# Two transformer blocks on one core: the wide projections turned from stationary to streaming weights

## What is computed

```python
h = rmsnorm(x, norm_g)                              # block 1
# attentions A (6 heads), C (4 heads), B (12 heads) give oa, oc, ob
g_a, g_b, g_c = split(sigmoid(h @ w_in[mix] + gate_bias), 3)
merged = g_a*(oa @ w_up_a) + g_b*(ob @ w_up_b) + g_c*(oc @ w_up_c)
x = x + merged @ w_o
h = concat([meta, x])                               # block 2, 16 + 256 tokens
u = rms_norm(h, g_pre_mix)
z_pool, v_conv, g_conv, gate_a, gate_b = split(u @ w_in_2)
y_a = pool(z_pool) @ w_pool_out                     # windows, a map per group
y_b = silu(layer_norm(conv31(v_conv * sigmoid(g_conv)))) @ w_conv_out
m = sigmoid(gate_a) * y_a + sigmoid(gate_b) * y_b
h = h + rms_norm(m @ w_o_2, g_post_mix)
u = rms_norm(h, g_pre_mlp)
h = h + rms_norm(square(relu(u @ w_up)) @ w_down, g_post_mlp)
```

## Time and profile before

| | us |
|---|---|
| median of 3 runs | 2298.14 (2297.1 to 2298.61) |
| profiled execution | 2297.23 |
| its span, first to last instruction | 2295.3 |
| PE busy | 2132.9 (93%) |
| PE weight loads | 1824.2 (79%) |
| DVE busy | 1590.3 (69%) |
| ACT busy | 966.8 (42%) |
| POOL busy | 418.4 (18%) |
| DMA | 384.46 MB, 167 GB/s |

### The profile page before, as it was taken

One profiled execution on the slowest core, in us unless ns is written; L12 is line 12 of the kernel. 1 busy time (PEld: TensorE's weight loads), 2 busy tenths in 40 slices (PEclk: granted clock), 3 DMA queues, 4 the chain that ended last, 5 costly groups with the idle time before them and its releaser, 6 DMA issues.

```text
span 2295.3 us, 33520 instructions
## 1 busy us (share of the span) xinstructions
PE 2132.9 (93%) x11733; PEld 1824.2 (79%) x11733; DVE 1590.3 (69%) x1828; ACT 966.8 (42%) x1197; POOL 418.4 (18%) x332
## 2 busy tenths in 40 slices
PE   6899999899998999799896999997999999999997
PEld 5767788788776888699775888776888888888886
DVE  6796876867876665646999867758645655655654
ACT  5443344566553444333232354445333333333343
POOL 3010010100213111102799402214000000000001
PEclk8899999999999999899998999998999999999999
DMA  7744555455446565355444545553556566556552
GB/s 233 223 124 139 149 165 160 133 155 166 138 138 188 169 202 186 122 181 157 139 148 133 175 137 183 183 183 128 183 192 189 186 192 193 183 193 192 185 185 89
DMA packets 345188, 384.46 MB, mean 167 GB/s; under 512 B 12359, under 2 KB 308213, under 8 KB 344679
## 3 DMA queue, kind: packets, MB, share of 16 engines
q1 hardware_dynamic: 341756, 370.95, 52.4%
q0 software_dynamic: 1120, 7.86, 1.0%
q10 hardware_dynamic: 2203, 4.23, 0.5%
HBM read 378.64 MB, written 4.23 MB: 167 GB/s over the span
## 4 chain that ended last, share of the span: by engine, by line
PE 67%; DVE 15%; POOL 8%; issue 5%; ACT 3%; DMA 1%; SPq 0%; DVEq 0%; POOLq 0%; ACTq 0%
PE acc L482 27%; PE acc L481 14%; PE acc L462 5%; PE acc L464 5%; PE acc L463 5%; DVE w_low L414 4%; POOL product L703 4%; PE acc L478 2%; POOL conv L705 2%; ACT w_high L406 2%; PE acc L472 2%; PE acc L474 2%; PE acc L473 2%; DVE tmp L499 2%; DVE conv L1735 1%
## 5 line engine op out<-in xcount | busy, mean ns | idle before, releaser
L414 DVE TENSOR_TENSOR w_low<-stage,w_high 128x1024 fp32r<-128x1024 f32 (+2 forms) x598 | 734.9, 1241 | 437.9 <-ACT w_high L406 423.8
L406 ACT ACTIVATE w_high<-stage 128x1024 fp32r<-128x1024 f32 (+2 forms) x598 | 606.0, 1023 | 749.9 <-PE acc L482 641.0
L482 PE MATMUL acc<-hT,w_high 128*128 128x512 f32 x1395 | 501.1, 398 | 0.0
L481 PE MATMUL acc<-hT,w_low 128*128 128x256 f32 x1395 | 406.3, 291 | 3.3 <-DVE w_low L414 3.3
L482 PE MATMUL acc<-u,w_high 128*128 128x512 f32 x960 | 344.9, 401 | 0.0
L482 PEld LDWEIGHTS acc<-hT,w_high 128*128 128x128 f32 x1395 | 264.8, 190 | 59.0 <-issue 3.4
L481 PEld LDWEIGHTS acc<-hT,w_low 128*128 128x128 f32 x1395 | 266.4, 191 | 18.0 <-issue 11.5
L481 PE MATMUL acc<-u,w_low 128*128 128x256 f32 x960 | 271.5, 283 | 1.8 <-DVE u L1374 1.8
L414 DVE TENSOR_TENSOR low_rows<-stage_rows,high_rows 128x1024 fp32r<-128x1024 f32 x128 | 158.6, 1242 | 156.8 <-ACT high_rows L406 156.4
L406 ACT ACTIVATE high_rows<-stage_rows 128x1024 fp32r<-128x1024 f32 x128 | 135.7, 1060 | 205.5 <-PE acc L464 177.3
L482 PEld LDWEIGHTS acc<-u,w_high 128*128 128x128 f32 x960 | 181.9, 189 | 42.3
(11 more groups left out here) (350 smaller groups left out, 3640.0 us busy)
## 6 DMA issues: line engine op xcount, KB each, us to landing
stage<-in_w_in SPq DMA_DIRECT2D x296, 512.0 KB, 3.7
stage<-in_w_up SPq DMA_DIRECT2D x128, 512.0 KB, 3.7
stage_rows<-in_w_down SPq DMA_DIRECT2D x128, 512.0 KB, 4.4
stage<-in_w_o SPq DMA_DIRECT2D x64, 512.0 KB, 4.5
stage<-in_w_mem_kv SPq DMA_DIRECT2D x16, 512.0 KB, 7.5
stage<-in_w_pool_out SPq DMA_DIRECT2D x16, 512.0 KB, 3.5
stage<-in_w_conv_out SPq DMA_DIRECT2D x16, 512.0 KB, 4.2
stage<-in_w_up_a SPq DMA_DIRECT2D x16, 384.0 KB, 3.3
```

Source lines behind the costliest of these rows:

```text
L406: act.activation(high[:, pr, 0:kt, 0:p.cols], src[:, slot, 0:kt, 0:p.cols], ACT.Copy).then_inc(high_done, 1)
L414: dve.tensor_tensor(low[:, pr, 0:kt, 0:p.cols], src[:, slot, 0:kt, 0:p.cols], high[:, pr, 0:kt, 0:p.cols].bitcast(F32), ALU.subtract).then ...
L481: pe.matmul(bk[:, 0:T], low, a, start=False, stop=False, skip_group_check=True)
L482: mm = pe.matmul(bk, high, both, start=False, stop=final, skip_group_check=True)
```

## The change

All gates, up-projections, w_o, w_pool_out, w_conv_out and w_o_2 take the form by rows, 512 columns a part (`by_rows`). Their products now lie with tokens on partitions:

- The bias of the mix gates varies along the row. POOL fetches it broadcast to 128 partitions, 512 columns at a time into a ring of two (`load_bias`); DVE adds it, ACT takes the sigmoid, DVE multiplies by the up-projection and adds. POOL has no merge left. Block 2's gates go from PSUM through ACT's sigmoid, scaled per token.
- merged, h1, m and h2 are needed by channels for the next matmul. PE transposes them, 8 pieces per row block (`turn_rows`, tables `MERGED_AT`, `RESIDUAL_AT`, `MIXED_AT`), and ACT and DVE split them out of PSUM (`high_turned` and `low_turned`; with the gain, `high_scaled` and `low_scaled`).
- A norm is one scalar per token on its partition: ACT squares a row block and accumulates. Block 2's first norm is applied after the products: values, gates and pools are multiplied by `rstd_bc`, which PE spreads from two diagonal matrices.
- x is read again from its input (no `spill_x`), g_post_mix and g_post_mlp are read as rows, two parameter loads at the start go, and the residual stays in rows to the end.
- Heads in w_up_a come every 4 slabs instead of 5, as the job has 44 slabs, not 48.

The diff, cut to its core:

```diff
-ROWS0 = [("gate_bias", 48), ("norm_g", 16), ("mem_norm_g", 16), ("g_pre_mix_2", 16), ("g_post_mix_2", 16), ("g_pre_mlp_2", 16)]
-ROWS1 = [("g_post_mlp_2", 16), ("pool_scale_2", 8), ("b_dw_2", 8), ("conv_ln_g_2", 8), ("conv_ln_b_2", 8), ("kv_norm_g", 2),
+ROWS0 = [("norm_g", 16), ("mem_norm_g", 16), ("g_pre_mix_2", 16), ("g_pre_mlp_2", 16)]
...
-                   "w_up_a": {5 + 5 * h: 6 + h for h in range(8)},
+                   "w_up_a": {4 + 4 * h: 6 + h for h in range(8)},
                    "w_up_c": {3 + 4 * h: 14 + h for h in range(8)}}
-        META_AT = 8
+        META_AT = 4
+        UP_B, HEADS_END = 11, 44
+        MERGED_AT = {"w_up_b": {UP_B * r + 12: r for r in range(3)}, "w_o": {1: 3}}
+        RESIDUAL_AT = {"w_o": {8 * r + 9: r for r in range(3)}, "values": {0: 3}}
+        SQUARES_AT = {"w_o": {8 * r + 8: r for r in range(3)}, "values": {0: 3}}
+        MIXED_AT = {"conv_out": {4 * r + 5: r for r in range(3)}, "w_o_2": {1: 3}}
...
+        def by_rows(w, col0, slabs, lhs, ready=None):
+            return Part(w, col0, slabs, None, ready, cols=ROW, stride=ROW, rows=lhs)
...
-        for w, b, slabs, before in (("w_up_a", 0, [3, 3], 0), ("w_up_c", 2, [2, 2], 3), ("w_up_b", 1, [3, 3], 5)):
-            order.append((w, Job(8, [Part(A["w_in"], MIX + b * D, full, rhs_of(hT)),
-                                     Part(A[w], 0, slabs, rhs_of(o_pair), ("o_split", before))], 4)))
-        order += [
-            ("w_o", Job(8, [Part(A["w_o"], 0, full, rhs_of(merged_pair), ("merged_ready", 0))], 2)),
-        ]
+        for w, b, slabs, before in (("w_up_a", 0, 3, 0), ("w_up_c", 2, 2, 3), ("w_up_b", 1, 3, 5)):
+            order.append((w, Job(4, [by_rows(A["w_in"], MIX + b * D, [2] * 8, hT),
+                                     by_rows(A[w], 0, [2] * slabs, o_pair, ("o_split", before))], 4)))
+        order.append(("w_o", Job(4, [by_rows(A["w_o"], 0, [2] * 8, merged_pair, ("merged_ready", 0))], 2)))
...
-            ("conv_gates", Job(8, [Part(A["w_in_2"], POOL_W + 2 * CONV_W + D, full, u_tokens)], 2)),
+            ("conv_gates", Job(4, [by_rows(A["w_in_2"], POOL_W + 2 * CONV_W + D, [2] * 8, u_rows)], 2)),
             ("pool_grp", Job(4, [Part(A["w_pool_grp_2"], 0, [2], rhs_of(d_pair), ("d_ready", 0), stride=0)], 8)),
-            ("pool_out", Job(8, [Part(A["w_in_2"], POOL_W + 2 * CONV_W, full, u_tokens),
-                                 Part(A["w_pool_out_2"], 0, [4, 4], rhs_of(y_pair), ("y_pair_ready", 0))], 4)),
-            ("conv_out", Job(8, [Part(A["w_conv_out_2"], 0, [4, 4], rhs_of(conv_pair), ("conv_ready", 0))], 4)),
-            ("w_o_2", Job(8, [Part(A["w_o_2"], 0, full, rhs_of(m_pair), ("m_ready", 0))], 2)),
+            ("pool_out", Job(4, [by_rows(A["w_in_2"], POOL_W + 2 * CONV_W, [2] * 8, u_rows),
+                                 by_rows(A["w_pool_out_2"], 0, [2] * 4, y_pair, ("y_pair_ready", 0))], 4)),
+            ("conv_out", Job(4, [by_rows(A["w_conv_out_2"], 0, [2] * 4, conv_pair, ("conv_ready", 0))], 4)),
+            ("w_o_2", Job(4, [by_rows(A["w_o_2"], 0, [2] * 8, m_pair, ("m_ready", 0))], 2)),
...
-            pool.dma_start(spill_x, turned[:]).then_inc(s("x_out"), 16)
...
+            def load_bias(n):
+                branch, r = (0, 2, 1)[n // 4], n % 4
+                if n < 2:
+                    pool.wait_ge(s("head_stats"), NORMS_ALL)
                 else:
-                    repeat(pool, job.steps, 1, body, link, 1 if add else 0)
+                    pool.wait_ge(s("gate_in"), 2 * (n - 1))
+                cols = slice(branch * D + r * ROW, branch * D + (r + 1) * ROW)
+                pool.dma_start(bias_ring[:, n % 2, :], A["gate_bias"][cols].partition_broadcast(P)).then_inc(s(f"bias_in{n % 2}"), 16)
...
+            def high_scaled(pair, q, bank, first_col, gain, turned_sem, done):
+                act.wait_ge(s(turned_sem), q + 1)
+                for a in range(2):
+                    k = 2 * q + a
+                    act.activation(pair[:, k, 0, first_col:first_col + T], aux[:, bank, a * T:(a + 1) * T], ACT.Copy,
+                                   scale=column(gain, k)).then_inc(s(done), 1)
...
+            def residual_squares(name, n):
+                r = SQUARES_AT[name].get(n)
+                if r is None:
+                    return
+                for t in range(2):
+                    e = 2 * r + t
+                    act.wait_ge(s("h1_rows"), e + 1)
+                    if e >= 2:
+                        act.wait_ge(s("h1_squared"), e - 1)
+                    act.activation(square[:, t, 0:ROW], h_rows[:, t, r * ROW:(r + 1) * ROW], ACT.Square,
+                                   accum_out=sums_1[:, t, r:r + 1]).then_inc(s("h1_squared"), 1)
...
+            def turn_rows(rows, q, bank, done):
+                for a in range(2):
+                    k = 2 * q + a
+                    for t in range(2):
+                        mm = pe.transpose(aux[:, bank, (2 * a + t) * P:(2 * a + t + 1) * P], rows[:, t, k * P:(k + 1) * P], ident[:])
+                mm.then_inc(s(done), 1)
...
+                if n == 2:
+                    pe.wait_ge(s("diag"), 3)
+                    pe.matmul(aux[:, 1, 0:META], ones[0:META, :], meta_diag[:], start=True, stop=True)
+                    for t in range(2):
+                        mm = pe.matmul(aux[:, 1, META + t * P:META + (t + 1) * P], ones[:], diag[:, t, :], start=True, stop=True)
+                    mm.then_inc(s("rstd_spread"), 1)
...
+            def turn_h2(r):
+                pe.wait_ge(s("h2_rows"), 2 * r + 2)
+                for q in (2 * r, 2 * r + 1):
+                    if q >= 4:
+                        pe.wait_ge(s("pair_ready"), 24 + q - 3)
+                    turn_rows(h_rows, q, q % 4, "h2_turned")
...
+            def low_scaled(pair, q, bank, first_col, gain, high_sem, first):
+                dve.wait_ge(s(high_sem), 2 * q + 2)
+                for a in range(2):
+                    k = 2 * q + a
+                    ins = dve.scalar_tensor_tensor(out=pair[:, k, 1, first_col:first_col + T], in0=aux[:, bank, a * T:(a + 1) * T], scalar=column(gain, k),
+                                                   in1=pair[:, k, 0, first_col:first_col + T].bitcast(F32), op0=ALU.mult, op1=ALU.subtract)
+                    link.put(ins)
+                dve.wait_ge(dve_link, link.n)
+                dve.sem_inc(s("pair_ready"), 1)
...
+                    if part == 0:
+                        dve.wait_ge(s(f"bias_in{n % 2}"), 16 * (n // 2 + 1))
+                        if n:
+                            dve.wait_ge(s("sig_ready"), 2 * n)
+                        for t in range(2):
+                            dve.tensor_tensor(tmp[:, t, 0:ROW], banks[:, t, :], bias_ring[:, n % 2, :], ALU.add).then_inc(s("gate_in"), 1)
+                        dve.wait_ge(s("gate_in"), 2 * n + 2)
+                        dve.sem_inc(acc_free, 1)
+                        return
+                    dve.wait_ge(s("sig_ready"), 2 * n + 2)
+                    for t in range(2):
+                        if n0 == 0:
+                            dve.tensor_tensor(merged[:, t, cols], banks[:, t, :], gate[:, t, 0:ROW], ALU.mult).then_inc(s("gate_used"), 1)
+                        else:
+                            link.put(dve.tensor_tensor(gate[:, t, 0:ROW], banks[:, t, :], gate[:, t, 0:ROW], ALU.mult))
...
+                    for t in range(2):
+                        dve.tensor_tensor(merged[:, t, cols], merged[:, t, cols], gate[:, t, 0:ROW], ALU.add).then_inc(s("gate_used"), 1)
...
-                dve.wait_ge(s("residual"), g + 1)
-                fold(dve, tmp[:, u, 0:2 * T].rearrange("p (a t) -> p a t", a=2), banks).then_inc(s("folded"), 1)
-                dve.wait_ge(s("folded"), g + 1)
+                r = 2 * i + u
+                cols = slice(r * ROW, (r + 1) * ROW)
+                if r == 0:
+                    dve.wait_ge(s("x_back"), 16)
+                for t in range(2):
+                    dve.tensor_tensor(h_rows[:, t, cols], banks[:, t, :], x_rows[:, t, cols], ALU.add).then_inc(s("h1_rows"), 1)
...
-            dve.wait_ge(s("residual"), 2 + 8)
-            inverse_std(TM, 1.0 / D, EPS)
-            normalize(lambda k: h1[:, k, :], uT, TM, "g_pre_mix_2", 16, rstd[:, 0:TM])
...
+                if n == 0:
+                    dve.wait_ge(s("h1_squared"), 8)
+                    link(dve.tensor_reduce(rs_1, sums_1, AX, ALU.add))
+                    dve.tensor_scalar(rs_1, rs_1, 1.0 / D, EPS, ALU.mult, ALU.add).then_inc(s("var_1"), 1)
+                if n == 1:
+                    dve.wait_ge(s("root_1"), 1)
+                    dve.reciprocal(rs_1, rs_1).then_inc(s("rs_1"), 1)
+                    dve.wait_ge(s("rs_1"), 1)
+                    for t in range(2):
+                        dve.tensor_scalar(diag[:, t, :], ident[:], rs_1[:, t:t + 1], None, ALU.mult).then_inc(s("diag"), 1)
```

(26 more changed lines are left out.)

564 lines of the change are left out of this document (294 added, 270 removed).

## The result

| | before | changed |
|---|---|---|
| median | 2298.38 us (2297.1 to 2301.11, 4 runs) | 2199.14 us (2197.62 to 2200.72, 4 runs) |
| span of the profiled execution | 2295.3 | 2197.5 |
| mean granted clock | 0.970 | 0.984 |
| PE busy, matmuls | 2132.9 (93%) | 2101.2 (96%), 10667 |
| DVE busy | 1590.3 | 1490.8 |

The ratio is 0.9567 (95% interval 0.955 to 0.9583): 99 us or 4.3% faster. The forecast was 2214, so the direction and the range held, and the gain was underestimated by 15 us.

A forecast was written before the change was run, and what follows sets the result against it. PE, busy 93% of the span, was taken to bind through its stream of weight slabs and the places where it stops. Stage terms summed to -83.0 us, from 2297.2 to 2214, range 2195 to 2230.

The forecast's parts named there:

- Mix stage: w_up_a, w_up_c, w_up_b: streaming 348.8, heads 40, transposes 2.8 and waits 6 make 397.6 us, a change of -30.4.
- The form: Tokens stationary, weights streaming, 12 matmuls a slab instead of 16: worth 3.2 us per 2048x2048 matrix, 25 us in all.
- worth nothing: Rival: the 3.2 us came from w_up1's folds and splits, so streamed gates keep the old pace, 2239 us; chance 0.13.
- Gap before block 2: The 17.01 us before `values`: the scale is applied after the product, so `values` starts at once; -15 us.
- conv_gates: Stage bound by DVE, not PE: eight folds go to ACT as sigmoids, the taps stay; -9.7 us.
- conv_out: Stage conv_out: -1.6 us for half a matrix in the new form, +2.8 for 24 transposes; +1.2.
- w_o_2: Stage w_o_2: -3.2 us for the form, +0.9 for 8 transposes, half its excess of 2.6 let go; -3.6.
- w_up0: Stage w_up0: 16 transposes add 1.9 us, less 1.4 for a supply that keeps ahead; +0.5.
- Gap before w_up0: The 18.14 us before w_up0: a new chain of 13 operations takes about 9 us; -9, ends -12 and -4.
- The start: Two of six parameter loads ahead of PE's first transpose go; -1 us, ends -1.5 and 0.
- half the waits return: Rival: mix stage keeps its 26 us beyond stream and heads, and `values` starts no earlier; 2249 us, chance 0.12.
- slower: Rival: sigmoid waits and turned-block stops at 32 places cost 3.56 us each, 114 in all; 2328 us, chance 0.04.

The follow-up runs named there:

- 16-matmul run: Changed kernel with each streamed low-weight product made in two matmuls of 256 columns, 16 matmuls a slab instead of 12: 2220.43 us.
- three edits: Changed kernel with convolution taps in tile pairs from `gates` on (2189.94 us), then the `d_ready` wait behind conv_gates (2186.74), then taps spread over pool_out: 2183.38 us.

## Why the prediction was right, and where it was off

- **Mix stage**, 397.6 forecast, 399.09 measured. The sum of bare stream, heads, transposes and 6 us of waits held; POOL's chain of 736.93 is gone and the DVE wait of 436.26 stayed, as said; whether the chain went because the merge left POOL or because it is due four slabs later, no run separates. That the broadcasts of the bias cost nothing held too, as no wait names them.
- **The form.** A slab of a streamed gate takes 2.72 us (445.55 to 448.27), as said. The 3.2 us a matrix were put down to a fixed part per matmul; the 16-matmul run shows 2.1 of them, and leaves 1.2 open. The rival "worth nothing" falls, but up to 1.2 us a matrix of it may be true.
- **Gap before block 2**, -15 forecast, -15.1 measured. The 2 us wait expected at the diagonals is 0.6 (L1330), with 0.7 before the last row block of h1 is turned.
- **conv_gates**, -9.7 forecast, -10.0 measured, and DVE is still full. "pool_grp is untouched" was wrong: -3.1. The folds put back undid both, so the step was the same eight folds, priced at their own length when they cost 1.6 us each. The 3.35 us that the forecast read for DVE's slab adds lengths that overlap; from split to split a slab without a fold takes 2.95 (1160.55 to 1163.50 before the change), and the sum of the time did not use it.
- **pool_out**, -12.8 and -13.8. The wait at 1286.10 went with POOL's merge; that is read from the rows, no run put the merge back.
- **w_o**: +0.5 forecast, -0.4 measured. **w_down3**: -3.7 and -3.7, 32 transposes at 0.117 us; the run with 128 more gave 0.116.
- **conv_out** +1.2 against -1.2, **w_o_2** -3.6 against -4.9: one fault in both. I left standing what they had over bare stream and transposes. After the change there is nothing over: 43.6 + 24 x 0.117 = 46.4 for the first (46.27 measured), 87.2 + 0.9 = 88.1 for the second (87.95).
- **w_up0**, +0.5 against -3.9, the largest miss. I let it keep most of its excess of 6.3 us. That excess was mostly one wait, for pieces of u that DVE had not scaled yet, and 3.9 us of missing clock (0.96 of 96.69) around it:

```profile
1570.78 0.38 PE L481 MATMUL acc<-u,w_low 128*128 128x256 f32 x1 [1.77 <-DVE u L1374]
```

  Now PE does not wait in w_up0, and 0.9 us of clock is missing (0.99 of 92.83), so the stage is the bare 90.35 and 16 transposes. That the shorter chain brought both is a reading of the rows; no run put it back.
- **Gap before w_up0**, -9 forecast, -7.8 measured. The chain is as described, and 10.3 us long instead of 9; warming PE took 0.45 off it.
- **The start**, -1 against -4.7. I costed the loads and did not look at the write of 2 MB, since nobody waits for it soon. It delayed the 36 KB that DVE does wait for. The two parts together account for 3.0 by the medians; the rest is open.

The rival "half the waits return" has no row for it, and "slower" needed 2.6 us at each of 32 places; the 6.1 us before w_up0 apart, which the forecast had as a gap of its own, the largest wait found there is 0.7. The 15 us by which the gain was larger are the start (3.7), pool_grp (3.1), conv_out (2.4), w_up0 (4.4), and smaller ones of both signs. The range held them all, but the four largest misses lie on the same side: each is an old cost that the forecast let stand, or a saving that it did not look at.

## What to carry to other kernels

Where PE is full, the time of a stage is the bare stream plus what PE itself does besides (transposes at their own length); when an edit takes away the engine that came late, forecast the stage at that sum and don't let an old excess stand. Where another engine is full, move its work to a stage where it has room and its neighbour is idle (15.8 us here, in three edits), and see that nothing piles up ahead of a later due point. When a large transfer goes, look for the small ones near it that somebody waits for.

## What was unexpected of the hardware

- VectorE and GpSimd lose time beside each other, and whichever instruction falls there pays. Per slab of conv_gates the split and its taps took 1.21 and 1.89 us (three taps), 1.21 and 1.57 (two), 1.76 and 1.09 (two, in another phase). With GpSimd idle three taps take 1.26. VectorE counts as busy throughout (96.06 of 99.97 us, 90.53 of 90.78), so a busy share near 1 isn't all work.
- 36 KB written to DRAM from ACT's queue took 5.4 us to land when 2 MB had gone out on POOL's queue 5 us earlier (61.4), and less than 2.9 without.
- Products put into PE's idle time made the transposes after them 1.7 times as fast (3.68 us for sixteen, then 1.09 for eight), and of that 0.45 us came off the gap.
